# Gated-DeltaNet row broadcasts through DRAM, values before the last subtractions, first output tiles split earlier

## What is computed

```python
beta = jax.nn.sigmoid(dn_b)
g = -jnp.exp(a_log) * jax.nn.softplus(dn_a + dt_bias)
gc = jnp.cumsum(g.reshape(b, h, n, c), axis=-1)
decay = where(incl, exp(gc[..., :, None] - gc[..., None, :]), 0.0)
a_mat = where(strict, einsum('bhnid,bhnjd->bhnij', kc * bc, kc) * decay, 0.0)
rhs = concatenate([vc * bc, kc * bc * exp(gc)[..., None]], axis=-1)
sol = triangular_solve(eye(c) + a_mat, rhs, lower=True, unit_diagonal=True)
intra = einsum('bhnid,bhnjd->bhnij', qc, kc) * decay
# and then a scan over the chunks, an RMSNorm, a gate silu(z), and the output projection
def swiglu_ffn(x, w_in, w_out):
    gate, up = jnp.split(x @ w_in, 2, axis=-1)
    return (jax.nn.silu(gate) * up) @ w_out
```

## Time and profile before

| | us |
|---|---|
| median of 3 runs | 2419.82 (2419.26 to 2423.41) |
| profiled execution | 2425.94 |
| its span in the profile | 2424.2 |
| PE busy | 2368.8 (98%) |
| DVE busy | 1563.2 (64%) |
| ACT busy | 1126.5 (46%) |
| POOL busy | 29.6 (1%) |
| granted TensorE clock, mean | 0.995 of full speed |

### The profile page before, as it was taken

One profiled execution on the slowest core, in us unless ns is written; L12 is line 12 of the kernel. 1 busy time (PEld: TensorE's weight loads), 2 busy tenths in 40 slices (PEclk: granted clock), 3 DMA queues, 4 the chain that ended last, 5 costly groups with the idle time before them and its releaser, 6 DMA issues.

```text
span 2424.2 us, 32228 instructions
## 1 busy us (share of the span) xinstructions
PE 2368.8 (98%) x12361; PEld 2028.6 (84%) x12361; DVE 1563.2 (64%) x2101; ACT 1126.5 (46%) x1516; POOL 29.6 (1%) x69
## 2 busy tenths in 40 slices
PE   8999999999999999999999999999999999999998
PEld 8999988778888888888879888787888888888886
DVE  6657775577666666655587666766766666666556
ACT  4345554564444444444465445545444444444443
POOL 1000000100000000000000000000000000000000
PEclk9999999999999999999999999999999999999999
DMA  7555521645555555655545652335555555555553
GB/s 263 191 174 174 172 105 55 257 161 193 198 195 193 190 191 191 225 191 194 196 164 180 241 174 87 102 122 195 176 196 195 189 198 190 190 210 207 192 194 115
DMA packets 180090, 437.99 MB, mean 181 GB/s; under 512 B 7232, under 2 KB 19632, under 8 KB 165920
## 3 DMA queue, kind: packets, MB, share of 16 engines
q1 hardware_dynamic: 177984, 425.75, 50.7%
q0 software_dynamic: 2016, 11.02, 1.2%
HBM read 434.64 MB, written 2.10 MB: 180 GB/s over the span
## 4 chain that ended last, share of the span: by engine, by line
PE 90%; DVE 5%; ACT 3%; issue 1%; DMA 0%; SPq 0%; DVEq 0%; ACTq 0%
PE bank L1856 28%; PE bank L1857 28%; PE bank L1858 28%; PE bank L2108 2%; PE bank L2345 1%; DVE w_lo L1134 1%; ACT w_hi L640 1%; PE bank L2318 1%; PE bank L2083 1%; DVE stats L1211 1%; DVE x L1210 1%; DVE spare_lo L1134 0%; PE bank L2336 0%; ACT yt L714 0%; DVE yt L1234 0%
## 5 line engine op out<-in xcount | busy, mean ns | idle before, releaser
L1134 DVE TENSOR_TENSOR w_lo<-raw,w_hi 128x1024 fp32r<-128x1024 f32 x776 | 944.6, 1224 | 733.7 <-ACT w_hi L640 731.7
L640 ACT ACTIVATE w_hi<-raw 128x1024 fp32r<-128x1024 f32 x776 | 820.0, 1060 | 1075.7 <-PE bank L1858 1066.6
L1856 PE MATMUL bank<-w_hi,xt_hi 128*128 128x512 f32 x1904 | 748.2, 393 | 2.5 <-DVE xt_lo L1242 1.2
L1858 PE MATMUL bank<-w_hi,xt_lo 128*128 128x512 f32 x1904 | 743.2, 390 | 0.0
L1857 PE MATMUL bank<-w_lo,xt_hi 128*128 128x512 f32 x1904 | 743.1, 390 | 0.0
L1856 PEld LDWEIGHTS bank<-w_hi,xt_hi 128*128 128x128 f32 x1904 | 358.9, 188 | 77.1 <-issue 1.9
L1858 PEld LDWEIGHTS bank<-w_hi,xt_lo 128*128 128x128 f32 x1904 | 358.6, 188 | 75.0
L1857 PEld LDWEIGHTS bank<-w_lo,xt_hi 128*128 128x128 f32 x1904 | 359.0, 189 | 73.2
L1856 PE MATMUL bank<-xt_hi,w_hi 128*128 128x256 f32 x928 | 267.4, 288 | 9.8 <-DVE w_lo L1134 9.8
L1856 PE MATMUL bank<-w_hi,a_hi 128*128 128x512 f32 x672 | 261.7, 390 | 2.1 <-DVE a_lo L1184 2.1
L1857 PE MATMUL bank<-xt_lo,w_hi 128*128 128x256 f32 x928 | 263.4, 284 | 0.0
(11 more groups left out here) (277 smaller groups left out, 1489.7 us busy)
## 6 DMA issues: line engine op xcount, KB each, us to landing
raw<-in_ffn_w_in_dram SPq DMA_DIRECT2D x176, 1024.0 KB, 4.9
raw<-in_ffn_w_out_dram SPq DMA_DIRECT2D x88, 1024.0 KB, 4.8
raw<-in_hy_w_in_dram SPq DMA_DIRECT2D x53, 1024.0 KB, 4.9
raw<-in_nsa_w_in_dram SPq DMA_DIRECT2D x41, 1024.0 KB, 5.0
raw<-in_hy_w_out_dram SPq DMA_DIRECT2D x16, 1024.0 KB, 4.9
raw<-in_nsa_w_out_dram SPq DMA_DIRECT2D x16, 1024.0 KB, 5.1
raw<-in_hy_w_in_dram SPq DMA_DIRECT2D x8, 512.0 KB, 8.6
raw<-in_cmp_w_k_dram SPq DMA_DIRECT2D x4, 1024.0 KB, 5.8
```

What stands on the lines that cost most here:

```text
L640: act.activation(weights_of(h)[0], half_of(h), ACT.Copy).then_inc(w_hi_ready, 1)
L1134: dv.tensor_tensor(lo, half_of(h), hi.bitcast(F32), ALU.subtract).then_inc(w_lo_ready, 1)
L1856: pe.matmul(dst, l_hi, r_hi, start=start, stop=False, skip_group_check=shared)
L1858: return pe.matmul(dst, l_lo, r_hi, start=False, stop=stop, skip_group_check=shared)
```

## The change

- PE's `row` and `beta` products are taken out. Instead DVE copies the gc rows (PE makes them by one more small matmul, 16 x 128) to `gc_row`, POOL writes them to DRAM (`gc_rows`, 8 KB), waits, and reads them back spread over the 128 partitions, 1 MB, into the tile where the exponentials are taken. Beta goes the same way at the start of the convolution part, where ACT now takes its sigmoid, both for the rows and for `sm`.
- `decays` runs after the sixth half, not the fifth, and DVE's handling of gc and ACT's exponentials of gc are moved into the last chunk. ACT's halves there are 3, then SiLU and the exponentials, then 2, where they were 5.
- DVE waits for the gc broadcast, adds -gc and the triangle for all four units in a row (L1495), before the four units; ACT takes the four exponentials in a row, and the units' halves follow.
- `values` is moved ahead of the last level's subtractions. PE's `corrected` now also waits for those subtractions.
- FFN: ACT's last loop round is written out; the first two output tiles are split after the sixth half of the last chunk, and wait only for pair 0's hT. DVE splits them between the 14th and 15th turn of the last pair but one.

```diff
+            pool.wait_ge(from_act, 1)
+            by_head = beta_rows.rearrange("(t h) j -> h t j", t=NT)
+            pool.dma_start(by_head, beta_feature[16:24, :].rearrange("h (t j) -> h t j", t=NT)).then_inc(beta_out, 16)
+            pool.wait_ge(beta_out, 16)
+            pool.dma_start(dn_more[:, 1, :], bcast(beta_rows.rearrange("m j -> (m j)"), NT * DNH * P)).then_inc(beta_in, 16)
+            pool.wait_ge(gc_row_ready, 1)
+            pool.dma_start(gc_rows, gc_row).then_inc(gc_out, 16)
+            pool.wait_ge(gc_out, 16)
+            pool.dma_start(dn_more[:, 0, :], bcast(gc_rows.rearrange("m j -> (m j)"), NT * DNH * P)).then_inc(gc_in, 16)
...
-                act.wait_ge(hT_ready, PAIRS * (layer + 1) - 1)
+                act.wait_ge(hT_ready, PAIRS * layer + 1)
                 for kt in range(2):
                     split(kt)
-                halves(1)
+                halves(3)
+                act.wait_ge(hT_ready, PAIRS * (layer + 1) - 1)
...
-                loop_over(5, 32, body)
+                loop_over(4, 32, body)
+                for n in range(PAIRS - 2, PAIRS):
+                    halves(8)
+                    gate(c0 + 2 * n, n)
+                    halves(8 if n < PAIRS - 1 else 6)
...
+                        done(act.activation(beta_feature, ba_out[P - 32:P, :], ACT.Sigmoid))
+                        wait_sp_read(act, ("ba",))
+                        done(act.activation(sm[:, 2, :].rearrange("p (t h) -> p t h", t=NT), sm[:, 0:2, 0:8], ACT.Sigmoid))
...
-                        halves(5)
+                        halves(3)
...
+                    if m == 5:
+                        act.wait_ge(for_act, 10)
+                        done(act.activation(sm[:, 6, :], sm[:, 4, :], ACT.Exp))
+                        done(act.activation(sm[:, 14, 8:16], sm[:, 14, 8:16], ACT.Exp))
+                        halves(2)
...
+            dv.wait_ge(gc_in, 16)
+            for t, hh in units:
+                Dt = tiles_of(t, hh)[0]
+                for h in range(4):
+                    n = 8 * t + 4 * hh + h
+                    ins = dv.scalar_tensor_tensor(Dt[:, h, :], Dt[:, h, :], ngc[:, n:n + 1], neg_lower[:, :], ALU.add, ALU.add)
+                to_act(ins)
...
-                sp_out(dv.tensor_tensor(AT, AT, sp4(("beta", t, hh)), ALU.mult), ("beta", t, hh))
+                to_act(dv.tensor_tensor(AT, AT, E, ALU.mult))
...
             for n in range(len(BLOCKS)):
+                if n == len(BLOCKS) - 1:
+                    for t, hh in units:
+                        values(t, hh)
...
-                    after = {5: decays}
+                    after = {6: decays}
...
-                for name, row in (("row", 4), ("beta", 2)):
-                    by_head((name, t, hh), lambda h: sm[:, row, m + h:m + h + 1].to_broadcast([P, P]), lambda h: ident[:, :])
...
                     handed(("rhs", t, hh))
+                    wait_sp_read(pe, ("x", t, len(BLOCKS) - 1, hh))
                     by_head(("v", t, hh), lambda h: X[:, h, :], lambda h: T[:, h, :])
```

More of the change, by code:

```diff
@@ L284, in trunk @@
         for t, hh in units:
[L285 removed]
+            uses([("kk", t, hh), ("kq", t, hh)])
         for n in range(len(BLOCKS)):
@@ L401, in trunk @@
         hands([("g",)])
-        hands([("rows",)] + [("base", t, hh) for t, hh in units])
+        hands([("base", t, hh) for t, hh in units])
         for n in range(1, len(BLOCKS)):
@@ L883, in _ @@
             halves(1)
-            for t, hh in units:
-                wait_sp_read(act, ("row", t, hh))
+            for n, (t, hh) in enumerate(units):
+                act.wait_ge(for_act, 11 + n)
                 dt_ = tiles_of(t, hh)[0]
                 done(act.activation(dt_, dt_, ACT.Exp))
+            for n, (t, hh) in enumerate(units):
                 halves(1)
-                wait_sp_read(act, ("beta", t, hh))
+                act.wait_ge(for_act, 15 + n)
                 for q in range(P // 32):
@@ L1340, in ffn @@
                 for n in range(PAIRS - 1):
-                    for k in range(16):
+                    for k in range(16 if n < PAIRS - 2 else 14):
                         halves(1)
@@ L1347, in last_up @@
                 def last_up():
+                    for k in (14, 15):
+                        halves(1)
+                        turn(PAIRS - 2, k)
                     up(PAIRS - 1)
@@ L1542, in _ @@
                     z_scaled(0)
-            def values(t, hh):
-                T = tiles_of(t, hh)[3]
-                return dv.tensor_tensor(T, v_tok[:, t, 4 * hh:4 * hh + 4, :], over(beta[:, heads_of(t, hh)], DH), ALU.mult)
-            for hh in range(2):
-                to_pe(values(0, hh), ("rhs", 0, hh))
             for kt in range(3):
                 early_split("out0", kt)
-            for hh in range(2):
-                own(values(1, hh))
             z_scaled(1)
@@ L2064, in decays @@
                 pe.matmul(b[:, 0:16], upper[:, :], sm[:, 3, :], start=True, stop=True)
+                pe.matmul(b[0:NT * DNH, P:2 * P], sm[:, 3, :], upper[:, :], start=True, stop=True)
                 sp_done(pe.matmul(b[:, 16:24], ones[:, :], sm[:, 3, 0:8], start=True, stop=True), ("gc",))
```

80 lines of the change are left out of this document (40 added, 40 removed).

## The result

| | before | changed |
|---|---|---|
| median of the runs, us | 2421.61 (2419.26 to 2423.80, 4 runs) | 2405.77 (2405.32 to 2407.30, 4 runs) |
| ratio, with 95% interval | | 0.9934 [0.9919, 0.9949] |
| profiled execution: time, span, mean granted clock | 2425.9, 2424.2, 0.995 | 2407.3, 2405.5, 0.997 |

The changed kernel is 15.8 us faster, 12 to 20 us by the interval. The forecast was 2401.0 with a range of 2397 to 2409, so the sign and the range held. The number lies in the case that the prediction called the late broadcast (2403 to 2411, chance 0.28), not in its likeliest case (2397 to 2403, chance 0.62). So the range held, but the likeliest case did not come true.

What follows compares the result with a forecast made beforehand. The prediction took PE's work to bound the kernel. Gains of 13.5 us up to the diagonal blocks, 3.5 for the values and 2.1 for the FFN sum to 19.1, from 2419.8 to 2400.7, said as 2401; range 2397 to 2409.

Steps and rivals of the forecast that it cites:

- the late broadcast: Rival: the gc broadcast lands late, PE waits at the diagonal blocks; 2403 to 2411 us, chance 0.28.
- likeliest case: First case, all terms hold, with the rival of a clock falling all the same included; 2397 to 2403 us, chance 0.62.
- The products: Row and beta products taken off PE in four DeltaNet units: 7.1 us, net 6.9 after the added gc matmul.
- the decays: Decays after the sixth half: PE's wait of 1.52 us for g goes, gain 1.5 us.
- ScalarE's order: ACT's SiLU and exponentials earlier, ahead of the transposes: PE's waits of 0.75 and 2.76 us go, gain 3.5 us.
- The base bound: DVE's chain from broadcast landing to diagonal blocks: 36.4 us, PE starts at 341.4, no gain lost, none to spare.
- T: Time the gc broadcast has landed: 305.0, from issue at 295.8, write 2.5, wakes 0.2, read 6.5 us.
- each us of T beyond 305 costs one: Rival's rule: the chain behind the broadcast's landing becomes the bound, each later us delays the diagonal blocks by one.
- The values: Values ahead of last subtractions: 2.52 us wait and 1.4 of clock go, 0.4 returns on `xt_lo`; net 3.5 us.
- The FFN: Earlier splits ahead of the output projection: PE's wait of 1.07 us for `a_lo` goes in each layer, 2.1 us.
- The clock: PE's clock falls avoided behind waits: 1.6 us at 309, 1.4 us behind the values' wait.
- The rule cited from the Trainium skill: Transposes don't count as busy; 24 in a row could let PE's clock fall without a wait, gain 1.6 us smaller.

Runs made afterwards that it cites:

- no_bcast: Kernel before plus only the moved values and the FFN change, keeping its own broadcasts by PE; 2415.82 us, ratio to before 0.9969.
- row_at_once: Changed kernel with the second broadcast reading beta's row at once, no write of the decays' row, so wrong decays; 2404.83 us, ratio to before 0.9919.
- reorder: Changed kernel with DVE's beta step, product of k by decays and one weight half ahead of its broadcast wait; 2402.45 us, ratio to before 0.9914.
- dead_products: Changed kernel with 32 useless PE products, 8 ahead of each unit's kk products, standing for those removed; 2411.85 us, ratio to before 0.9951.
- second_write: Changed kernel with the decays' row written to DRAM twice, one behind the other, ahead of its broadcast; 2407.32 us, ratio to before 0.9935.
- act_order: Changed kernel with ACT's two weight halves back in front of the sixth chunk's exponentials; 2406.41 us, ratio to before 0.9939.
- again: The changed kernel unaltered, run again as the yardstick of the follow-up set; 2405.97 us, ratio to before 0.9927.
- reorder3: reorder2 with DVE's gating of the second token tile ahead of a weight half; 2400.95 us, ratio to before 0.9917.
- reorder2: reorder with the output's first three splits on DVE ahead of the weight half behind the last subtractions; 2403.75 us, ratio to before 0.9926.

## Why the prediction came out as it did

**The products, the decays and ScalarE's order: right in sum.** The step said 13.5 us for PE's arrival at the blocks, with the clock. Measured are 11.2 us (no_bcast, and before), plus the 2.7 to 2.8 us that the late broadcast withheld (row_at_once, reorder): 13.9 us. The 7.1 us of products are confirmed by dead_products and row_at_once (4.43 and 2.79). The waits of 1.52, 0.75 and 2.76 us are gone; the terms of 1.5 and 3.5 us for them were not measured one by one.

**The base bound: the step that failed.** Its form was right: the blocks begin at T + 36.4. DVE's row gives T = 309.24, so 345.6, and PE begins at 345.33; second_write moved T by 2.3 us and the blocks by 2.35. But T was put at 305.0. The row was issued when the step said, 295.8 on before's axis (297.65 less 1.8). The write took 3.3 us in place of 2.5, with a wake of 0.3 us behind it, and the read 7.9 in place of 6.5, so T was 307.4 on that axis, 2.4 us late. The bounds had the write; the read came out at their upper end. The read was put below the median of the layer norm's rows with one weight slab beside it, and the case against a late landing was argued with the DMA share of 0.36 at 309 to 314. That is the stretch behind the transfers. The ones under them could be read in the trace of before as well (same columns as above):

```profile
295.80:299.50 3.70, 3.70 (x33) 3.70 (x32) 1.23 (x1) 1.06 (x1) 0.00 (x0) 1.00 0.70 262
299.50:303.50 4.00, 3.25 (x28) 3.07 (x27) 2.16 (x3) 3.77 (x4) 0.00 (x0) 1.00 0.77 262
303.50:307.50 4.00, 1.65 (x16) 1.41 (x13) 1.18 (x7) 3.80 (x7) 0.00 (x0) 1.00 0.02 5
```

The write ran in the first. The read was issued near the start of the second, in which before moves one weight slab (262 GB/s for 4.0 us, 1 MB), and the third is empty. So "one weight slab beside it" was right; the price of it was not. In the changed kernel the two share the DMA engines. The table of DMA queues (packets, MB, share of the 16 engines) for 301.3 to 309.2 has both, the slab in q1 and POOL's read in q0:

```profile
q1 hardware_dynamic: 518, 1.03, 45.8%
q0 software_dynamic: 144, 1.05, 32.1%
```

The same transfer of beta, issued at 181.8, took 1.7 us for the write and 4.8 for the read, and the read of `second_write` 5.0. In both stretches (181.7 to 186.6, and 304.7 to 309.7) the table has no q1, only the read; here the row of beta's, then that of `second_write`:

```profile
q0 software_dynamic: 144, 1.05, 56.7%
```

```profile
q0 software_dynamic: 144, 1.05, 59.6%
```

So the read costs 4.8 to 5.0 us alone, and beside one slab 7.0 to 7.9 in the eight traces whose DMAs are the changed kernel's (6.8 in `act_order`, which issues it later into the same slab). The prediction's 6.5 lay between the two. No row of before holds such a pair, and the median of the layer norm's loads, 7.9 us, is what the read took. By the Trainium skill's page "DMA: Bandwidth & Descriptors", "Anatomy of one DMA" (2.0 us fixed and the bytes at 436 GB/s), it would have been 2.0 and 4.4 us, an estimate by that page. That is near the beta pair, and 4.8 us short in sum for the pair that counted.

**What it cost: under-sized, too.** Of the three waits the trace shows 1.7 us, and taking them away brought 2.7. The prediction's "each us of T beyond 305 costs one" held for T (2.4 us late, 2.7 lost, with PE's own arrival 0.4 us earlier than counted; in second_write 2.3 us more, 2.35 lost), but the waits are no measure of it: see below.

**The values: right.** The step said 3.5 us net, with 0.4 as a new wait on `xt_lo`. Undoing it cost 3.43 us, of which the fall is some 1.6. The new wait was 0.66 us, not 0.4.

**The FFN: right, a little low.** 2.1 us were forecast; the trace gives 1.37 and 1.41, together 2.8.

**The clock: half of it was not seen.** The sum had the falls at 309 and behind the values' wait (1.6 and 1.4 us). Before has three more, at 439, 1466 and 1568. The first cost 1.5 us by the table (15.90 less 14.37), and neither trace of the changed kernel has it. The other two are not gone for good: placed by the splits, `again` has its fall at 1450 where before has that of 1466, and the first trace has its own at 1551 where before has that of 1568. The term was left out since no edit stands near these places. In the other direction, both traces of the changed kernel have a fall near 1307 that before has not, which costs nothing. The rule cited from the Trainium skill ("TensorE: Matmul & The Clock Gate", Part 4), by which the 24 transposes might let the clock fall, did not come true here: behind 2.94 us of transposes without a wait the granted clock stays at 1.00, in the stretch of 309.2 to 312.7 and up to 1309.

**The sum.** 19.1 us were forecast. The table gives 20.4 us between before and `again`. Four of before's falls have no partner of equal cost in `again`, about 6 us (an estimate: 1.6 and 1.4 as the sum had them, 1.5 at 439, 1.6 at 1568), and the rest, 14.4, is work and waiting. The forecast had 3.0 for falls and 16.1 for the rest, of which the late broadcast took 2.7, while the FFN brought 0.7 more. In the medians the difference is 15.8 to 17.6 us, because the average execution of before has fewer falls than the profiled one (its runs at a mean clock of 0.998 take 2419.5 to 2421.0, those at 0.995 2423.7 to 2426.6). Runs at the same mean clock of 0.998 say the same as the table: the changed kernel's take 2404.7 to 2406.1, 14 to 15 us less. The forecast took the profile's falls in full from a median that doesn't hold them all; that, the late broadcast and the second median of before, 1.8 us higher than the first, make up the 4.8 us between 2401.0 and 2405.77. The range held because it was wide enough for a late broadcast, and in part by luck: the sum took 3.0 us of falls from a median without knowing how many falls that median holds.

## What to carry to other kernels

A value that goes through DRAM to be broadcast is priced by the DMA traffic at the moment of its two transfers, so look which other transfers are on their way in just those stretches, and put everything that needn't wait for the landing ahead of it on the waiting engine: here three lines moved by one place brought back nearly all that the late landing had cost (2.69 of 2.79 us). Where a clock fall costs as much as the edit (1.4 to 1.7 us here), compare traces at the same instruction of a long, regular series instead of comparing medians, and count the falls apart. Place each fall by that series too, since times on two axes hide that two falls stand at the same place.

## What the runs showed of the hardware

**A wait costs more than it shows.** Removing waits of 1.67 us (0.46, 0.17 and 1.04) brought 2.7 us, and waits of 1.07 us in the FFN cost 1.4, in both layers. PE's timelines show where the rest is. Without a wait the next product begins before the modelled end of the one ahead, and a unit's 8 products, 16 records, are one row of 1.95 us, here in `reorder`:

```profile
313.79 0.48 PE L1886 MATMUL bank<-w_hi,xt_hi 128*128 128x512 f32 x1
...
316.61 1.95 PE L2139 MATMUL bank<-big 128*128 128x128 f32 x16
318.31 0.48 PE L1886 MATMUL bank<-w_hi,xt_hi 128*128 128x512 f32 x1
```

With the waits, in `again`, they are two rows of 1.16 us, and from one weight half to the next it takes 5.68 us in place of 4.52, for 0.63 us of shown waiting:

```profile
313.05 0.48 PE L1886 MATMUL bank<-w_hi,xt_hi 128*128 128x512 f32 x1
...
316.49 1.16 PE L2139 MATMUL bank<-big 128*128 128x128 f32 x8 [0.46 <-DVE gb L1527]
317.82 1.16 PE L2139 MATMUL bank<-big 128*128 128x128 f32 x8 [0.17 <-DVE dn_more L1531]
318.73 0.48 PE L1886 MATMUL bank<-w_hi,xt_hi 128*128 128x512 f32 x1
```

So the two waits add 0.53 us to what they show, and the third, at the blocks, some 0.5 (1.03 us for the three). In the FFN it is 0.3 us for each.

**The same transfer, issued later, can land sooner in its own time.** The 1 MB read took 7.7 us when issued at once, beside a weight slab, and 5.0 us when issued behind a second write, with no slab beside it. So 5.0 us of delay in the issue became 2.3 us at the landing.

**Where a clock fall is free.** It costs 1.4 to 1.75 us in dense work and nothing where PE would have waited anyway. At the fall near 1307 of `again` (PE busy for 3.46 of 3.50 us at the low level) the table shows no step. `reorder3` has the same stretch of the program at 1302.3, at the full clock; DVE is busy for 3.37 of 3.40 us in it, PE for 3.08, and PE waits for DVE's `w_lo` at either end, 2.30 and 0.38 us:

```profile
1302.30:1305.70 3.40, 3.08 (x24) 2.88 (x24) 3.37 (x4) 1.28 (x2) 0.00 (x0) 1.00 0.55 178
```

**The falls stand at few places of the program, each behind waits of PE.** The thirteen traces have 30 falls ahead of the program's end. Placed by the splits, they stand at seven places, near 309, 319, 387 (398 in before), 425 (439 in before), 1307, 1450 (1466) and 1551 (1568). Ahead of each, PE's timeline has one or more waits, the longest of them 0.9 to 2.8 us. Such a wait doesn't always bring a fall: at 425 PE waits 0.99 us for `yt` ahead of the fall of before (its 439), and as long in `again`, which has none. That place has a fall in five traces: before, dead_products, row_at_once, reorder and reorder2. Four of these are the kernels in which a wait ahead of the blocks was taken away, so it looks as if less waiting brought the fall; but before, with its waits of 2.76 and 2.52 us, has the fall as well, and reorder3, without waits ahead of the blocks, has it not. What decides is not shown. The fall at 425 is why 2.7 us won in the trace of reorder came out as 0.8 us at its end.
